# Latent attention with 64 and 32 rotary columns of the heads stored apart, and its scores in halves and quarters of the array, four heads at a time

## What is computed

```python
MLA_HEADS, MLA_NOPE, MLA_ROPE, MLA_VD = 16, 64, 32, 64
def mla_queries(cq, w_q_up, q_g):
    return rms_norm((cq @ w_q_up).reshape(B, L, MLA_HEADS, MLA_QK), q_g)      # MLA_QK = 96
def mla_keys_values(ckv, kpe, w_kv_up, k_g):
    kv = (ckv @ w_kv_up).reshape(B, L, MLA_HEADS, MLA_NOPE + MLA_VD)
    k_nope, v = kv[..., :MLA_NOPE], kv[..., MLA_NOPE:]
    k_pe = jnp.broadcast_to(kpe[:, :, None, :], (B, L, MLA_HEADS, MLA_ROPE))
    return rms_norm(jnp.concatenate([k_nope, k_pe], axis=-1), k_g), v
def mha(q, k, v, scale):                    # per block of 128 queries
    a = softmax_f32(jnp.einsum('bqhd,bkhd->bhqk', qb, k), scale)
    return jnp.einsum('bhqk,bkhv->bqhv', a.astype(v.dtype), v)
```

## Time and profile before

| | |
|---|---|
| three runs, median | 1520.59 us (1519.58 to 1520.69) |
| the profiled execution | 1519.7 us, its span 1517.5 us |
| PE busy | 1509.8 us |
| DVE busy | 1080.2 us |
| ACT busy | 668.4 us |
| POOL busy | 31.8 us |
| DMA traffic | 258.00 MB, 170 GB/s on average |

### The profile page before, as it was taken

How to read it: one execution, slowest core, us unless ns; L and a number is a source line. 1 busy time by engine, 2 the same in 40 slices (tenths; PEclk the granted TensorE clock), 3 DMA queues, 4 the chain that set the end, 5 groups by cost and what they waited for, 6 DMA issues and landing times.

```text
span 1517.5 us, 21930 instructions
## 1 busy us (share of the span) xinstructions
PE 1509.8 (99%) x8854; PEld 1443.9 (95%) x8854; DVE 1080.2 (71%) x1738; ACT 668.4 (44%) x1030; POOL 31.8 (2%) x43
## 2 busy tenths in 40 slices
PE   9999999999999999999999999999999999999999
PEld 5999999988779999999999999999997899999999
DVE  5887887788687887886678887877588876443332
ACT  5433333254686633333363333325458765333221
POOL 0000000000021000000000000000020000000000
PEclk9999999999999999999999999999999999999999
DMA  9756566543224355655455656654331033433333
GB/s 390 279 212 233 208 245 225 187 152 117 92 70 157 136 217 212 228 199 183 164 197 184 233 203 224 220 195 147 115 130 57 1 136 115 139 112 139 99 131 118
DMA packets 52132, 258.00 MB, mean 170 GB/s; under 512 B 6592, under 2 KB 8896, under 8 KB 36800
## 3 DMA queue, kind: packets, MB, share of 16 engines
q1 hardware_dynamic: 49344, 252.61, 46.0%
q10 hardware_dynamic: 2688, 4.00, 0.8%
HBM read 253.29 MB, written 3.29 MB: 169 GB/s over the span
## 4 chain that ended last, share of the span: by engine, by line
PE 95%; DVE 1%; ACT 1%; DMA 1%; issue 1%; SPq 0%; POOL 0%; ACTq 0%; DVEq 0%; POOLq 0%
PE ps L2103 29%; PE ps L2104 29%; PE ps L2105 29%; PE ps L2744 1%; PE ps L2464 1%; PE ps L2635 1%; PE ps L2753 1%; PE ps L2767 1%; PE ps L2490 1%; DMA wm_first<-in_w_mod_first 1%; DMA w_raw<-in_w_in 0%; PE ps L2212 0%; DVE w_lo L1319 0%; PE ps L2428 0%; PE ps L2235 0%
## 5 line engine op out<-in xcount | busy, mean ns | idle before, releaser
L1319 DVE TENSOR_TENSOR w_lo<-w_raw,w_hi 128x2048 fp32r<-128x2048 f32 (+3 forms) x178 | 349.6, 1966 | 236.7 <-ACT w_hi L749 234.0
L2103 PE MATMUL ps<-hx_hi,w_hi 128*128 128x384 f32 (+1 forms) x1432 | 480.2, 335 | 0.1
L2104 PE MATMUL ps<-hx_lo,w_hi 128*128 128x384 f32 (+1 forms) x1432 | 478.6, 334 | 0.0
L2105 PE MATMUL ps<-hx_hi,w_lo 128*128 128x384 f32 (+1 forms) x1432 | 478.6, 334 | 0.0
L749 ACT ACTIVATE w_hi<-w_raw 128x2048 fp32r<-128x2048 f32 (+3 forms) x178 | 294.7, 1656 | 404.4 <-DMA w_raw<-in_w_out 214.4
L2103 PEld LDWEIGHTS ps<-hx_hi,w_hi 128*128 128x128 f32 x1432 | 268.9, 188 | 2.4 <-issue 1.8
L2104 PEld LDWEIGHTS ps<-hx_lo,w_hi 128*128 128x128 f32 x1432 | 268.9, 188 | 0.0
L2105 PEld LDWEIGHTS ps<-hx_hi,w_lo 128*128 128x128 f32 x1432 | 268.8, 188 | 0.0
L2105 PE MATMUL ps<-g_hi,w_lo 128*128 128x384 f32 x704 | 236.6, 336 | 0.0
L2103 PE MATMUL ps<-g_hi,w_hi 128*128 128x384 f32 x704 | 236.5, 336 | 0.0
L2104 PE MATMUL ps<-g_lo,w_hi 128*128 128x384 f32 x704 | 236.5, 336 | 0.0
(11 more groups left out here) (280 smaller groups left out, 1476.8 us busy)
## 6 DMA issues: line engine op xcount, KB each, us to landing
w_raw<-in_w_in SPq DMA_DIRECT2D x88, 1024.0 KB, 4.8
wm<-in_w_mod SPq DMA_DIRECT2D x128, 512.0 KB, 5.7
w_raw<-in_w_out SPq DMA_DIRECT2D x64, 704.0 KB, 4.1
w_raw<-in_w_qkv SPq DMA_DIRECT2D x12, 1024.0 KB, 4.7
wm_first<-in_w_mod_first SPq DMA_DIRECT2D x8, 1024.0 KB, 19.2
w_raw<-in_w_o SPq DMA_DIRECT2D x8, 1024.0 KB, 4.9
w_raw<-in_w_qup SPq DMA_DIRECT2D x8, 576.0 KB, 3.7
w_raw<-in_w_down SPq DMA_DIRECT2D x6, 704.0 KB, 3.9
```

The lines of the kernel that those rows point to most:

```text
L1319: nc.vector.tensor_tensor(w_lo[:, slot, 0:width], w_raw[:, slot, 0:width], w_hi[:, slot, 0:width].bitcast(F32), ALU.subtract).then_inc(w_l ...
L2103: nc.tensor.matmul(out, l_hi, r_hi, start=first, stop=False)
L2104: nc.tensor.matmul(out, l_hi, r_lo, start=False, stop=False)
L2105: return nc.tensor.matmul(out, l_lo, r_hi, start=False, stop=last)
```

## The change

The plain and the rotary columns of the heads are stored apart, so that transposes always turn full blocks of 128 columns: two heads' plain columns (`mqN`, `mkN`) or four heads' rotary ones (`mqR`, `mkR`). A q chunk's four transposes per block become three (two of plain columns, one of rotary), each into all 128 partitions; per half of the keys there are four banks of plain and two of rotary transposes instead of eight. Scores then are sums of two products. `scores_nope(g, half)` multiplies 64 rows, two heads in two halves of the array, and `scores_rope(g)` adds 32 rows, four heads in four quarters of it, into four banks. The core thus works in 8 groups of four units, which are four heads: even groups with two score pieces, odd ones with one piece. The rotary part of a group is one burst, and `ms_ready` is raised for all four units by it. In PE's queue the two halves bursts of the next group stand ahead of the transposes of units 0 and 1 and of units 2 and 3 of this one, and `values` is cut into two parts. ACT's and DVE's queues follow. The q scaling of DVE becomes two instructions, and the rotary columns of the later keys move to POOL.

```diff
-            mqT = sb("mqT", [QK, MLA_HEADS, T], where=part)
+            mqN = sb("mqN", [P, MLA_HEADS // 2, T], where=part)
+            mqR = sb("mqR", [P, MLA_HEADS // 4, T], where=part)
...
+        mkN = mkT[:, 0:8, :]
+        mkR = mkT[:, 8:12, :]
...
             if t < 12:
-                return mqT[:, 4 * (t // 3):4 * (t // 3) + 4, (t % 3) * P:(t % 3 + 1) * P]
-            g, slot = divmod(t - 12, 4)
-            return mkT[0:QK, 4 * g:4 * g + 4, slot * P:(slot + 1) * P]
+                return (mqN[:, 2 * (t // 3) + t % 3, :] if t % 3 < 2 else mqR[:, t // 3, :]), ps[:, TURN_BANK[t], 0:T]
+            half, j = divmod(t - 12, 6)
+            if j < 4:
+                return (mkN[:, 4 * half:4 * half + 4, j * P:(j + 1) * P],
+                        ps[:, TURN_BANK[t], :].rearrange("p (h t) -> p h t", h=4))
+            return (mkR[:, 2 * half:2 * half + 2, 2 * (j - 4) * P:(2 * (j - 4) + 2) * P],
+                    ps[:, TURN_BANK[t], :].rearrange("p (h t) -> p h t", h=2))
...
-            return 2 * (u // 4) + u % 2
+            return 4 * (u // 8) + u % 4
 
         def mla_pieces(u):
 
-            return PIECES[(u // 2) % 2]
+            return PIECES[(u // 4) % 2]
 
         def mla_exps(u):
 
-            return 6 * (u // 4) + (2, 4, 5, 6)[u % 4]
+            return 12 * (u // 8) + (2, 4, 6, 8, 9, 10, 11, 12)[u % 8]
...
+            pool.wait_ge(kbank_free, 4)
+            for slot in range(1, 4):
+                ins = nc.gpsimd.tensor_tensor(mk_rope(1, slot).rearrange("p (g e) -> p g e", g=8),
+                                              kpg[:, slot, :].unsqueeze(1).to_broadcast([P, 8, ROPE]),
+                                              rinv[:, 8 * slot - 8:8 * slot].unsqueeze(2).to_broadcast([P, 8, ROPE]),
+                                              ALU.mult)
+            ins.then_inc(mkheads, 1)
...
+                exps(3)
+                evac(18)
+                evac(19)
+                for g in range(U // 4):
+                    evac_aT(4 * g)
+                    evac_aT(4 * g + 1)
+                    if g == 0:
+                        evac(20)
+                        evac(21)
+                    evac_aT(4 * g + 2)
+                    if g < U // 4 - 1:
+                        exps(4 * g + 4)
+                    evac_aT(4 * g + 3)
+                    if g == 0:
+                        evac(22)
+                        evac(23)
+                    elif g == 2:
+                        high_half(PHASE["wo", 1][0], 1)
+                    if g < U // 4 - 1:
+                        for u in range(4 * g + 5, 4 * g + 8):
+                            exps(u)
                 high_of("wo", 1, 1)
                 high_of("wo", 1, 2)
 
...
+                for g in range(U // 4):
+                    top(4 * g)
+                    if g == 0:
+                        key_nope(1, 3)
+                    top(4 * g + 1)
+                    scale(4 * g)
+                    top(4 * g + 2)
+                    scale(4 * g + 1)
+                    if g == 2:
+                        v.wait_ge(mtr_ready, len(TURN_BANK))
+                    if g >= 2 and g % 2 == 0:
+                        out_copy(g - 2)
+                    top(4 * g + 3)
+                    scale(4 * g + 2)
+                    scale(4 * g + 3)
+                    if g >= 2 and g % 2 == 0:
+                        out_copy(g - 1)
+                    elif g == 1:
                         low_half(PHASE["wo", 1][0], 0)
...
+                    elif g == 3:
                         low_half(PHASE["wo", 1][0], 1)
...
+                out_copy(6)
+                out_copy(7)
...
-                    for i in range(4):
+                    for i in range(3 if t < 12 else 4):
                         if t < 12:
-                            src = mq[:, (t // 3) % 2, t % 3, i * QK:(i + 1) * QK]
+                            src = mq[:, (t // 3) % 2, i, (t % 3) * P:(t % 3 + 1) * P]
                         else:
-                            g, slot = divmod(t - 12, 4)
-                            src = mkn(g // 2, slot)[:, 4 * (g % 2) + i, :]
-                        mm = nc.tensor.transpose(ps[0:QK, TURN_BANK[t], i * P:(i + 1) * P], src, ident[:])
+                            half, j = divmod(t - 12, 6)
+                            if j < 4:
+                                src = mk_nope(half, j)[:, i * P:(i + 1) * P]
+                            else:
+                                src = mk_rope(half, 2 * (j - 4) + i % 2)[:, (i // 2) * P:(i // 2 + 1) * P]
+                        mm = nc.tensor.transpose(ps[:, TURN_BANK[t], i * P:(i + 1) * P], src, ident[:])
                     mm.then_inc(mtr_ready, 1)
...
-                def scores(u):
-                    h = mla_head(u)
-                    if u >= 4:
-                        pe.wait_ge(mexp_done, mla_exps(u - 4))
-                    for qb, at, slots in mla_pieces(u):
-                        n = len(slots) * P
-                        mm = nc.tensor.matmul(ps[:, u % 4, at:at + n], mqT[:, h, qb * P:(qb + 1) * P],
-                                              mkT[0:QK, h, slots[0] * P:slots[0] * P + n], start=True, stop=True)
-                    mm.then_inc(ms_ready, 1)
+                def scores_of(u, qT, kT, rows, qb, at, slots, start, stop):
+
+                    n = len(slots) * P
+                    return nc.tensor.matmul(ps[:, u % 4, at:at + n], qT[rows, qb * P:(qb + 1) * P],
+                                            kT[rows, slots[0] * P:slots[0] * P + n], start=start, stop=stop)
+
+                def scores_nope(g, half):
+
+                    u0 = 4 * g + 2 * half
+                    if g:
+                        pe.wait_ge(mexp_done, mla_exps(u0 - 3))
+                    for i, piece in enumerate(mla_pieces(u0)):
+                        for u in (u0, u0 + 1):
+                            pair = mla_head(u) // 2
+                            scores_of(u, mqN[:, pair, :], mkN[:, pair, :], slice(NOPE * (u % 2), NOPE * (u % 2 + 1)), *piece,
+                                      i == 0, False)
+
+                def scores_rope(g):
+
+                    for i, piece in enumerate(mla_pieces(4 * g)):
+                        for u in range(4 * g, 4 * g + 4):
+                            quad = mla_head(u) // 4
+                            mm = scores_of(u, mqR[:, quad, :], mkR[:, quad, :], slice(ROPE * (u % 4), ROPE * (u % 4 + 1)),
+                                           *piece, False, i == len(mla_pieces(u)) - 1)
+                            if i == len(mla_pieces(u)) - 1:
+                                mm.then_inc(ms_ready, 1)
...
+                for t in (12, 13, 14, 15):
+                    pe.wait_ge(*turned(t))
+                scores_nope(0, 0)
+                pe.wait_ge(kbank_free, 4)
+                scores_nope(0, 1)
+                pe.wait_ge(*turned(16))
                 pe.wait_ge(*turned(17))
...
+                scores_rope(0)
                 turn_of(10)
+                pe.wait_ge(mheads, 4)
                 pe.wait_ge(*turned(9))
                 turn_of(11)
...
+                pe.wait_ge(k0_keys, 2)
+                pe.wait_ge(*turned(10))
+                turn_of(18)
+                pe.wait_ge(*turned(11))
+                turn_of(19)
+                pe.wait_ge(kbank_free, 6)
+                for g in range(U // 4):
+                    if g:
+                        if g == 1:
+                            pe.wait_ge(*turned(22))
+                        values(2 * g - 2)
+                    if g < U // 4 - 1:
+                        scores_nope(g + 1, 0)
+                    if g:
+                        if g == 1:
+                            pe.wait_ge(*turned(23))
+                        values(2 * g - 1)
+                    turn(4 * g)
+                    turn(4 * g + 1)
+                    if g == 0:
+                        pe.wait_ge(*turned(18))
+                        turn_of(20)
+                        pe.wait_ge(*turned(19))
+                        turn_of(21)
+                    if g < U // 4 - 1:
+                        scores_nope(g + 1, 1)
+                        scores_rope(g + 1)
+                    turn(4 * g + 2)
+                    turn(4 * g + 3)
+                    if g == 0:
                         pe.wait_ge(mkheads, 2)
...
+                        pe.wait_ge(*turned(20))
+                        turn_of(22)
+                        pe.wait_ge(*turned(21))
+                        turn_of(23)
                 values(U // 2 - 2)
                 values(U // 2 - 1)
 
```

More of the change, by code:

```diff
@@ L117, in build_step @@
         with ExitStack() as part:
-            mk1a = sb("mk1a", [P, 3, 8, QK], where=part)
+            mk1a = sb("mk1a", [P, 3, 8 * QK], where=part)
         with ExitStack() as part:
@@ L123, in build_step @@
         with ExitStack() as part:
-            mk1b = sb("mk1b", [P, 8, QK], where=part)
+            mk1b = sb("mk1b", [P, 8 * QK], where=part)
         with ExitStack() as part:
```

(54 more changed lines are left out.)

142 lines of the change are left out of this document (48 added, 94 removed).

## The result

| | before | after |
|---|---|---|
| median of 5 runs | 1519.72 us (1519.58 to 1520.69) | 1537.29 us (1535.56 to 1538.17) |
| the profiled execution, its span | 1519.7 us, 1517.5 us | 1538.17 us, 1536.2 us |
| PE, DVE, ACT busy | 1509.8, 1080.2, 668.4 us | 1513.1, 1078.3, 666.6 us |

A forecast was written before the change was run, and what follows sets the result against it. PE, busy 99% of the span, was taken as the bound; the new order strings rounds on a chain, ending the core 14.6 us later: 1519.7 + 14.6 = 1534.3, plus 0.9 to the median, 1535.2 us; range 1527 to 1542.

The forecast's parts named there:

- The chain: Attention core: rounds strung from rotary burst to rotary burst through DVE and ACT, making PE wait; 14.6 us later, chance 0.83.
- 8.7 and 7.9: Core: forecast us per round over a group with two score pieces and over one with one piece.
- the tail: End of core: last four units through maximum, scale, transpose, copy and values, forecast at 7.3 us.
- a quarter to a third: Core: forecast share of the time that DVE and ACT would both be idle.
- under a wait that is there anyway: ACT, round 2: half of the weight rounding, 1 us, 0.3 seen, costed at nothing because a wait would cover it.
- the 1.0 us I had added for what my walk fell short: Core's end: the step-by-step walk of the old order ended 1.0 us short of 1204.52, so 1.0 was added.
- the last term: Whole kernel: 0.9 us added to get from the profiled execution to the median, 1534.3 to 1535.2 us.
- Rival (c): Core: granted clock falls to 1.2 GHz because PE stands; for half the core, 1547 us, chance 0.04.
- PE's own work, -2.5: PE in the core: transposes -3.1, scores -5.9, shape changes +6.5; inside the rounds, not seen apart.
- the 0.18 taken: PE in the core: us assumed per change of the array's shape, 36 more changes making +6.5 us.
- Rival (a): Core: DVE and ACT deliver in time, PE stays full; 1518.1 us, or 1514.8 with half-price shape changes, chance 0.08.
- Rival (b): Rotary scores: quarters don't run side by side, 18 us more, 1553 us, chance 0.05.

The follow-up runs named there:

- e4: Kernel before with the scores of four units issued as one burst that waits for the fourth exponential; storage, shapes, DVE and ACT queues unchanged: 1531.29 us.
- e2: Changed kernel with DVE's and ACT's queues reordered (maxima first, output copy and exponentials earlier, evacuations between first exponentials), PE's queue untouched: 1525.89 us.
- e8: Changed kernel's computation and storage with the queues of PE, DVE and ACT all reordered, differently in even and odd groups: 1522.29 us.
- e10: e9 with one more ACT edit: the rounding of the first weight panel's second half moved behind the third group's exponentials: 1531.28 us.
- e3: Changed kernel with dummy transposes of the identity into an idle bank where PE waits (first round, rounds 2 to 6): 1534.83 us.
- e9: Changed kernel with evacuations of q tiles 10 and 11 and key tiles 18 and 19 put between ACT's first four exponentials: 1533.01 us.
- e5: Kernel before with a one-column matmul of 32 rows added ahead of every unit's transposes, adding 64 changes of the array's shape: 1531.29 us.
- e6: Kernel before with the same added one-column matmul as e5, but of 128 rows: 1524.02 us.

## Why the prediction was right, and what it missed

- **The chain, forecast at 0.83, is the cause.** Three kinds of edit agree: put alone into the kernel before it costs 11.5 us (e4); taken down by the order of two engines' queues it gives 11.4 back (e2), of three 15.0 (e8), in each of which are some 3 us of the clock; and no instruction of PE differs between the changed kernel and e2.
- **The rounds.** "8.7 and 7.9": the three over an even group that carry nothing else took 8.75, 8.76 and 8.75 us, the odd one without other work 7.99. First score 1146.33 (forecast 1146.3), the first group 3.01 (3.0), the tail 7.55 (7.3), PE's idle time in the core 15.7 (15 to 20). DVE and ACT stood for 35 and 39% of the seven rounds, a little more than "a quarter to a third".
- **The mis-sized terms.** The seven rounds took 66.3 us, the forecast 61.5. The first two took 21.5 instead of 19.6 (8.7 + 7.9 + 3), of which 6.8 us ran at 1.2 GHz. The fourth took 10.56 instead of 7.9: 0.9 for the weight rounding, which I counted at nothing "under a wait that is there anyway" while it stands between two exponentials of the chain, as e10 shows, and the rest at 1.2 GHz. Less the 1.0 us I had added for what my walk fell short, and with 0.3 of the tail, the core ended 4.1 us later than forecast in the profiled execution (1223.22 against 1219.1).
- **Luck in the last term.** The sum forecast 14.6 us more than before; measured are 17.6 between the medians and 18.5 between the two profiled executions. The 0.9 us that I added from the profiled execution to the median came from three runs of before (1520.59); over five runs its median is 1519.72, that of the profiled execution. No mechanism stands behind that term, nor behind the 1.0 us for the walk, and both lay on the side of the miss. That is why the forecast is off by 2.1 us only.
- **Rival (c), the clock**, was forecast at 0.04 as half of the core at 1.2 GHz. It came as two stretches of some 6.8 and 3.4 us and cost some 3 us: 2.5 by e3, 2.2 and 3.4 by what e9 and e2 gained beyond the walk, and 1.84 for the second stretch alone in the profiled execution. My range had room for brief dips; the sum should have had a term for them once I forecast waits of 3 us in a stretch where PE had been full.
- **PE's own work, -2.5.** Not measured alone. e8's span is 2.5 us over that of before and its PE waits 3.7 us in nine places; with 0.2 us of draining and filling at each, which I took for a handing over, 5.5, less the 0.8 which the same count gives for before's one line. That leaves some -2.2. The term is consistent with the forecast, its parts are not settled: a change of shape cost 0.11 to 0.13 us (e5 less e6) against the 0.18 taken, and with 0.13 the same sum would give -4.3. (The prediction calls records matmuls: its 64 and 32 score matmuls are 32 and 16, of two records each. The sum is right.)
- **Rival (a)**, chain covered: false, though the orders of e8 come within 4.2 us of its 1518.1. **Rival (b)**, quarters one after the other: false. The quarters of four units took 1.07 us (1189.10 to 1190.17), as long as the halves of two (1188.03 to 1189.10); one after the other they would take twice 1.7. A one-piece burst took 0.86 us (1198.07 to 1198.93, the end of that row's stretch), a two-piece one 1.07, where full concurrency and 0.2 for the change made 0.84 and 1.05. By the 3.07x of the Trainium skill's page "TensorE: Matmul & The Clock Gate" (Part 3, Measured speedup vs the span model) quarters would, as an estimate, cost 1.3 times their share. The trace doesn't bear that out in what the second piece adds: 0.21 us for eight records of 128 columns, a quarter of 8 x 0.107, where 3.07x would make 0.28. For a whole burst it depends on what is taken for the change: with 0.11 and not 0.2 the two bursts come to 3.4 and 3.6 times.

## What to carry to other kernels

Packing four heads into the array's rows makes their score tiles finish and come free together. Before the column savings are counted, look for who lives between those two moments: with one PSUM bank per unit and four units per burst, maximum and exponential of all four stand in series with PE, and a full PE becomes a link of a chain. Then the order of the queues is worth more than the packing: 11.4 us by those of DVE and ACT alone and 15.0 by all three, some 3 of them through the clock, against some 2 us of PE's own work. And side work on DVE or ACT, harmless under a full PE, costs nearly its whole length if it stands ahead of a releasing instruction (0.9 of the rounding's 1.06 us).

## What the runs showed of the hardware

- PE's granted clock fell to 0.50 behind waits of 2.81 and 1.78 us and stayed there for 6.8 and 3.4 us although PE was busy again (3.50 of 3.50 us in the stretch from 1155.20). It did not fall in any run of e10_rounding_later, where the longest wait is 1.66 us, and not in some executions of e9_head with one of 1.78. What decides between them was not tried.
- 82 dummy transposes in the waits kept the granted clock at 1.00 and made a kernel 2.5 us faster.
- A matmul of one column with 128 rows, two records, took 0.14 us of PE's queue, more than a 128-column transpose of one record (0.11), and 0.31 with 32 rows between bursts of other shapes.
